# Attention with keys on the partitions: scores made transposed, row maxima from a separate one-pass product, denominators added up on GpSimd

## The reference, cut to what matters

```python
def block_attention(q, k, v):          # latent: 8 query heads, 2 key heads, head size 64, 2048 + 128 keys
    scale = HEAD_DIM ** -0.5
    def one_block(qblk):               # 128 queries
        s = jnp.einsum('bkgqd,bskd->bkgqs', qblk, k).astype(jnp.float32) * scale
        p = jax.nn.softmax(s, axis=-1).astype(v.dtype)
        return jnp.einsum('bkgqs,bskd->bkgqd', p, v)
```

## Time and profile before

| | |
|---|---|
| median of three runs | 3549.56 us |
| the profiled execution, its time | 3547.59 us |
| its span in the profile | 3545.8 us |
| TensorE busy, span | 3171.3 us (89%) |
| VectorE busy, span | 1878.6 us (53%) |
| ScalarE busy, span | 1671.7 us (47%) |
| GpSimd busy, span | 388.6 us (11%) |
| mean granted clock of TensorE | 0.939 of full speed |

### The profile page before, as it was taken

One profiled execution on the slowest core, in us unless ns is written; L12 is line 12 of the kernel. 1 busy time (PEld: TensorE's weight loads), 2 busy tenths in 40 slices (PEclk: granted clock), 3 DMA queues, 4 the chain that ended last, 5 costly groups with the idle time before them and its releaser, 6 DMA issues. The chain is left out here.

```text
span 3545.8 us, 60756 instructions
## 1 busy us (share of the span) xinstructions
PE 3171.3 (89%) x21856; PEld 2900.2 (82%) x21856; DVE 1878.6 (53%) x3485; ACT 1671.7 (47%) x3239; POOL 388.6 (11%) x400
## 2 busy tenths in 40 slices
PE   6999994759999999999699756999999999999991
PEld 6788883748888888888588645999999999999991
DVE  2222226548888888888533365545455445545443
ACT  2222220547777777777434202455455544455442
POOL 0333333500000000000000000010010000110001
PEclk9999997869999999999799855999999999999996
DMA  5121113410000000000244204565565555665545
GB/s 217 43 80 60 67 66 116 140 42 25 27 27 27 27 27 27 27 27 27 81 147 150 83 0 132 174 192 185 179 198 184 183 187 179 188 193 181 181 130 220
DMA packets 307599, 393.69 MB, mean 111 GB/s; under 512 B 13808, under 2 KB 263872, under 8 KB 306496
## 3 DMA queue, kind: packets, MB, share of 16 engines
q1 hardware_dynamic: 293680, 338.64, 28.9%
q0 software_dynamic: 10240, 35.66, 4.4%
q10 hardware_dynamic: 3600, 18.35, 1.3%
HBM read 318.68 MB, written 74.06 MB: 111 GB/s over the span
## 5 line engine op out<-in xcount | busy, mean ns | idle before, releaser
L2304 DVE TENSOR_TENSOR e_w_lo<-e_raw,e_w_hi 128x2048 fp32r<-128x2048 f32 x192 | 440.1, 2292 | 490.4 <-ACT e_w_hi L2246 490.4
L92 PE MATMUL e_ps<-e_x_hi,e_w_hi 128*128 128x272 f32 x2048 | 602.1, 294 | 5.5 <-issue 5.5
L94 PE MATMUL e_ps<-e_x_hi,e_w_lo 128*128 128x272 f32 x2048 | 593.8, 290 | 0.0
L93 PE MATMUL e_ps<-e_x_lo,e_w_hi 128*128 128x272 f32 x2048 | 590.1, 288 | 0.0
L2246 ACT ACTIVATE e_w_hi<-e_raw 128x2048 fp32r<-128x2048 f32 x192 | 366.1, 1907 | 163.7 <-DMA e_raw<-in_w_gate 159.3
L1470 DVE TENSOR_TENSOR a_pT_lo<-a_ps_t,a_pT_hi 128x512 fp32r<-128x512 f32 (+1 forms) x648 | 368.0, 601 | 139.5 <-ACT a_pT_hi L1368 139.2
L1368 ACT ACTIVATE a_pT_hi<-a_ps_t 128x512 fp32r<-128x512 f32 (+1 forms) x648 | 319.6, 532 | 185.1 <-PE a_ps_t L1238 180.5
L92 PEld LDWEIGHTS e_ps<-e_x_hi,e_w_hi 128*128 128x128 f32 x2048 | 386.1, 189 | 7.1 <-issue 5.5
L93 PEld LDWEIGHTS e_ps<-e_x_lo,e_w_hi 128*128 128x128 f32 x2048 | 386.9, 189 | 0.0
L94 PEld LDWEIGHTS e_ps<-e_x_hi,e_w_lo 128*128 128x128 f32 x2048 | 385.8, 188 | 0.0
L1443 DVE TENSOR_REDUCE a_mx<-a_ps_s 128x1 f32<-128x896 f32 (+2 forms) x392 | 346.1, 890 | 26.8 <-PE a_ps_s L1228 26.8
(11 more groups left out here) (269 smaller groups left out, 5478.2 us busy)
## 6 DMA issues: line engine op xcount, KB each, us to landing
e_raw<-in_w_gate SPq DMA_DIRECT2D x64, 1024.0 KB, 5.2
e_raw<-in_w_up SPq DMA_DIRECT2D x64, 1024.0 KB, 5.2
e_raw<-in_w_down SPq DMA_DIRECT2D x64, 1024.0 KB, 5.2
a_wm<-in_w_mod SPq DMA_DIRECT2D x32, 512.0 KB, 4.0
s_ret<-p_pr SPq DMA_DIRECT2D x17, 768.0 KB, 3.6
m_raw<-in_w_in ACTq DMA_DIRECT2D x8, 1152.0 KB, 7.1
o_cT<-s_ct SPq DMA_DIRECT2D x17, 512.0 KB, 4.7
s_x<-o_x SPq DMA_DIRECT2D x17, 512.0 KB, 4.9
```

The lines of the kernel that those rows point to most:

```text
L92: nc.tensor.matmul(out, w_hi, x_hi, start=first, stop=False)
L93: nc.tensor.matmul(out, w_hi, x_lo, start=False, stop=False)
L94: return nc.tensor.matmul(out, w_lo, x_hi, start=False, stop=last)
L2304: nc.vector.tensor_tensor(w_lo[n % RING][:, :, :], raw[n % RING][:, :, :], w_hi[n % RING][:, :, :].bitcast(F32), ALU.subtract).then_inc(w_ ...
```

## The change

The probabilities are now made with keys on the partitions, so nothing has to be transposed. The unit of work becomes a slot: one query tile and one key head, hence 4 heads times 128 queries = 512 columns (`QCOLS`). There are two slots in a tile. The 17 key tiles of a slot are taken in 9 pairs (`PAIRS`), the last of one tile only.

- `scores` uses a key tile as weights and 512 query columns as the moving side: two matmuls of 512 columns per key tile, one with k_hi over 128 rows, one with k_lo over 64 rows and a 65th row. That row is 1 in `keys_lo` and minus the query's maximum in `qM`, so the subtraction of the maximum is part of the sum, and `exps` needs no bias.
- The maximum must be known beforehand. `rough` makes one-pass scores (k_hi alone) with queries on the partitions, in 20 pieces of 448 or 384 columns per slot (`PIECE_W`), in two banks `ps_r`. VectorE reduces each (`maxima`), then the pieces (`tops`); TensorE turns the maxima into a row (`turn_top`), and ScalarE copies it with its sign changed (`keep_top`). All this runs one slot ahead, `PIECES_IN` pieces beside each pair.
- `exps` writes 128x1024 probabilities into a ring of three buffers (`prob`), `high` rounds them into `p_hi` on ScalarE, `low` writes the remainder to `p_lo` on VectorE. Both inputs of `low` are in SBUF.
- The denominators come from GpSimd: `add` sums the probabilities of all pairs into `acc` (seven instructions of 1024 columns, two of 512 a slot), and four small products with a column of ones in `fold_halves` finish the sum.
- `value` has 512 columns. All side work goes through one PSUM bank, `ps_m`.
- In the key loop ScalarE copies tile i - 1 (`keep_keys`, now two copies) after it has rounded tile i. Queries are loaded and split before the key loop.

```diff
-SEG_ORDER = [0, 2, 1]
-PIECES = [(0, 3), (3, 6), (6, 9), (9, 12), (12, 15), (15, KEY_TILES)]
-GROUP = 2
-NGRP = NQ // GROUP
+PAIRS = (KEY_TILES + 1) // 2
+PIECE_W = [448, 448, 448, 448, KEY_TILES * P - 4 * 448]
+PIECES = len(PIECE_W) * QPK
+PIECES_IN = [0, 3, 3, 3, 3, 3, 3, 2, 0]
+QCOLS = QPK * P
+QUADS = NKV * NT
+RING = 3
...
+            def add(i, v, r, out, x, y):
+                n = pair(i, v, 0) + r
+                if r:
+                    pool.wait_ge(folded, n)
+                nc.gpsimd.tensor_tensor(out, x, y, ALU.add).then_inc(folded, 1)
+
+            def body(i):
+                for v in range(NKV):
+                    pool.wait_ge(exped, pair(i, v, 1) + 1)
+                    add(i, v, 0, acc[:, :, :], prob[:, 0, :, :], prob[:, 1, :, :])
+                    for j in range(2, PAIRS - 1):
+                        pool.wait_ge(exped, pair(i, v, j) + 1)
+                        add(i, v, j - 1, acc[:, :, :], acc[:, :, :], prob[:, j % RING, :, :])
+                    if not first_slot(i, v):
+                        pool.wait_ge(filled, use_of_fold(*before(i, v)) + 1)
+                    add(i, v, PAIRS - 2, acc_all[:, :], acc[:, 0, :], acc[:, 1, :])
+                    pool.wait_ge(exped, pair(i, v, PAIRS - 1) + 1)
+                    add(i, v, PAIRS - 1, acc_all[:, :], acc_all[:, :], prob[:, (PAIRS - 1) % RING, 0, :])
+
+            slots(pool, body)
 
         @block.tensor
...
+            def rough(i, v, n):
+
+                if n == 0:
+                    pe.wait_ge(emptied, use_of_queries(i, v) + 1)
+                if not (first_slot(i, v) and n < 2):
+                    pe.wait_ge(max_ok, piece(i, v, n) - 1)
+                h, part = (n, 0) if ctx_tile(i) else (n // len(PIECE_W), n % len(PIECE_W))
+                w = P if ctx_tile(i) else PIECE_W[part]
+                src = CTX_KEYS * P if ctx_tile(i) else sum(PIECE_W[0:part])
+                nc.tensor.matmul(ps_r[n % 2][:, 0:w], qT[v][:, h * P:(h + 1) * P], keys[:, v, src:src + w],
+                                 start=True, stop=True).then_inc(rough_ok, 1)
...
+            def scores(i, v, j, t):
+
+                n = pair(i, v, j)
+                b = (v + j) % 2
+                if j == 0 and t == 0:
+                    pe.wait_ge(emptied, use_of_top(i, v) + 1)
+                    pe.wait_ge(qM_ok, quad(i, v) + 1)
+                if t == 0 and not (first_slot(i, v) and j < 2):
+                    pe.wait_ge(exped, n - 1)
+                src = CTX_KEYS if ctx_tile(i) else 2 * j + t
+                nc.tensor.matmul(ps_s[b][:, t, :], keys[:, v, src * P:(src + 1) * P], qT[v][:, :], start=True, stop=False)
+                ins = nc.tensor.matmul(ps_s[b][:, t, :], keys_lo[:, v, src * P:(src + 1) * P], qM[v][:, :],
+                                       start=False, stop=True)
+                if t == tiles_of(i, j)[-1]:
+                    ins.then_inc(scored, 1)
+
...
+            def slot(i, v):
+                last, ahead = before(i, v), following(i, v)
+                at = 0
+                for j in range(PAIRS):
+                    todo = list(range(at, min(at + PIECES_IN[j], pieces_of(ahead[0]))))
+                    at = at + PIECES_IN[j]
+                    if j == 0:
+                        if not first_slot(i, v):
+                            for t in range(2):
+                                value(*last, PAIRS - 2, t)
+                        turn_queries(*ahead)
+                    for t in tiles_of(i, j):
+                        scores(i, v, j, t)
+                        if todo:
+                            rough(*ahead, todo.pop(0))
+                    if j == PAIRS - 1:
+                        turn_top(*ahead)
+                    if j == 1 and not first_slot(i, v):
+                        value(*last, PAIRS - 1, 0)
+                    for t in range(2):
+                        if j >= 2:
+                            value(i, v, j - 2, t)
+                        if todo:
+                            rough(*ahead, todo.pop(0))
+                    if j == 2:
+                        modulation(i, v)
+                    if j == 3 and not first_slot(i, v):
+                        fold_halves(*last)
+                    if j == 5 and not first_slot(i, v):
+                        turn_out(*last)
 
             def body(i):
-                bank = Bank(i)
-                for h in range(NQ):
-                    uses_before = [bank.uses_of(b) for b in range(2)]
-                    for kind, n in step_events(i, h):
-                        if kind == "q":
-                            turn_queries(i + 1, n, bank)
...
+            def exps(i, v, j):
+
+                n = pair(i, v, j)
+                act.wait_ge(scored, n + 1)
+                if not (first_slot(i, v) and j < RING):
+                    act.wait_ge(lo_ok, PAIRS * (QUADS - 1) + 7 + v if ctx_tile(i) else n - RING + 1)
+                    done = {0: PAIRS * quad(*before(i, v)) + 6, 1: PAIRS * quad(*before(i, v)) + 7,
+                            2: PAIRS * quad(*before(i, v)) + 9}[j] if j < RING and not ctx_tile(i) else \
+                        PAIRS * (QUADS - 1) + 6 + v if ctx_tile(i) else PAIRS * quad(i, v) + max(j - RING, 1)
+                    act.wait_ge(folded, done)
+                m = len(tiles_of(i, j))
...
+            def high(i, v, j):
+
+                n = pair(i, v, j)
+                act.wait_ge(exped, n + 1)
+                if ctx_tile(i):
+                    act.wait_ge(valued, PAIRS * (QUADS - 1) + v + 1)
+                elif not first_slot(i, v):
+                    act.wait_ge(valued, n - PAIRS + 1)
+                m = len(tiles_of(i, j))
+                nc.scalar.activation(p_hi[:, place(i, v, j), 0:m, :], prob[:, place(i, v, j) % RING, 0:m, :], ACT.Copy)\
+                    .then_inc(hi_ok, 1)
...
+            def maxima(i, v, n):
+
+                dve.wait_ge(rough_ok, piece(i, v, n) + 1)
+                h, part = (n, 0) if ctx_tile(i) else (n // len(PIECE_W), n % len(PIECE_W))
+                w = P if ctx_tile(i) else PIECE_W[part]
+                nc.vector.reduce_max(mx[:, h, part:part + 1], ps_r[n % 2][:, 0:w], AX).then_inc(max_ok, 1)
+
+            def tops(i, v):
+
+                dve.wait_ge(max_ok, piece(i, v, pieces_of(i)))
+                if first_slot(i, v):
+                    dve.wait_ge(made, 2)
+                else:
+                    dve.wait_ge(filled, use_of_top(*before(i, v)) + 1)
+                n = 1 if ctx_tile(i) else len(PIECE_W)
+                nc.vector.reduce_max(top[:, :, HD:HD + 1].rearrange("p h o -> p (h o)"), mx[:, :, 0:n], AX).then_inc(top_ok, 1)
+
...
+            def low(i, v, j):
+
+                dve.wait_ge(hi_ok, pair(i, v, j) + 1)
+                m = len(tiles_of(i, j))
+                at = place(i, v, j)
+                nc.vector.tensor_tensor(p_lo[:, at, 0:m, :], prob[:, at % RING, 0:m, :], p_hi[:, at, 0:m, :].bitcast(F32),
+                                        ALU.subtract).then_inc(lo_ok, 1)
+
...
+            def slot(i, v):
+                last, ahead = before(i, v), following(i, v)
+                at = 0
+                for j in range(PAIRS):
+                    todo = list(range(at, min(at + PIECES_IN[j], pieces_of(ahead[0]))))
+                    at = at + PIECES_IN[j]
+                    if j == 3:
+                        keep_modulation(i, v)
+                    if j == 4 and not first_slot(i, v):
+                        combine(*last)
+                    if todo:
+                        maxima(*ahead, todo.pop(0))
+                    if j == 7:
+                        if todo:
+                            maxima(*ahead, todo.pop(0))
+                        tops(*ahead)
+                    if j:
+                        low(i, v, j - 1)
+                    elif not first_slot(i, v):
+                        low(*last, PAIRS - 1)
+                    for n in todo:
+                        maxima(*ahead, n)
+                    if j == 0:
+                        copy_queries(*ahead)
+                    if j == 4 and v == 0:
+                        queries_lo(i + 1)
 
```

641 lines of the change are left out of this document (280 added, 361 removed).

## The result

The changed kernel takes 3751.18 us (median of four runs, 3725.79 to 3772.18). The kernel before takes 3548.57 beside it, so the ratio is 1.057, 95% interval 1.0483 to 1.0657. The direction was as forecast. The size was not: 3597 us was expected, with 3680 as the upper end.

What follows compares the result with a forecast made beforehand. GpSimd additions and VectorE subtractions, excluding each other, were taken to bound a slot: 14.5 + 32 x 31.9 + 13 = 1048 us against 984.6, +64; key loop -14; +50 on 3547.6 gives 3597 us, range 3560 to 3635, reaching to 3515 and 3680.

Steps and rivals of the forecast that it cites:

- slots, 32: Attention's main part: 32 slots of 31.9 us each, against 29.6 for half a query tile before.
- prologue: From attention's last key copy to the first real scores: 14.5 us with nothing beside it, bounds 10 to 18.
- epilogue: End of attention with the context tile: three chains from value to copy, 4.4 us each, 13 us, bounds 10 to 18.
- key loop: Attention's loop over 16 key tiles: 1.9 us a tile instead of 2.84, so -14 us, bounds 0 and -20.
- rival B: In attention TensorE, 75% busy with gaps, runs a third of the slots' time at clock 0.50: 3680 us; 14%.
- the exchange: In slots, GpSimd additions and VectorE subtractions exclude each other: 30.8 - 2.1 + 3.2 = 31.9 us; 59%.
- the queue behind a blocked subtraction: In a slot, maxima wait behind the subtraction, then TensorE's rough products (two banks only), scores and values; no separate size.
- signs: In attention: POOL near 70%, adds 2.4 to 3.5 us, `a_p_lo` shortest 1.22, mean well above 1.7, TensorE clock 1.00.
- the queries' subtraction: VectorE's subtraction for new queries: half of it, 0.35 us, counted in each slot's sum.
- TensorE's own work: Per slot 24 us: 15.4 for 68 products of 512 columns, up to 4.5 rough products, about 4.5 side work.
- Rival A: In slots, no exclusion that counts: VectorE bounds a slot at 28 us, total 3472 us; 20%.

Runs made afterwards that it cites:

- e1: The changed kernel with GpSimd's additions cut to one column each, denominators left out: 3574.34 us, ratio 1.007.
- e5: e1 with seven unused 512-column products filling TensorE's long wait before the fourth rough product: 3494.44 us, ratio 0.985.
- e7: The changed kernel with three of TensorE's waits filled by products that change nothing (9, 7 and 5 of 512 columns): 3643.39 us, ratio 1.026.
- e4: The changed kernel with exponentials in place in the PSUM score buffer, subtraction reading one operand there, GpSimd adding only rounded parts: 3549.63 us, ratio 1.000.
- e2: The changed kernel with each GpSimd addition replaced by a one-column one and an SBUF fill of about equal length: 3577.49 us, ratio 1.008.
- e8: e4 with modulation products moved to the end of pair 1 and, in pair 7, VectorE's subtraction before its last two maxima and tops: 3464.23 us, ratio 0.976.
- e11: e4 with only the modulation products moved to the end of pair 1, VectorE's order in pair 7 kept: 3479.07 us, ratio 0.981.
- e10: The changed kernel with only the 16 modulation products moved from the end of pair 2 to pair 1: 3677.47 us, ratio 1.037.

## Why the prediction was wrong

The profiled executions differ by 3725.8 - 3547.6 = 178 us; the forecast was 50. Term by term:

| term | predicted us | measured us | off by |
|---|---|---|---|
| slots, 32 | 32 x 31.9 = 1021 | 1129.3 | +108 |
| of it at full clock | 31.9 | (31.4 + 33.7) / 2 = 32.55 | +21 |
| of it the half clock | 0 | 35.29 - 32.55 = 2.74 a slot | +88 |
| prologue | 14.5 | 761.0 - 742.9 = 18.1 | +4 |
| epilogue | 13 | 1920.1 - 1890.3 = 29.8 | +17 |
| key loop | -14 | 742.9 - 760.0 = -17.1 | -3 |

The sum of the last column without the two rows "of it", +126, and the forecast of 3597 make 3723 us; 3726 was measured.

**The step that failed: TensorE's clock.** The sum took all slots at clock 1.00, and the half clock stood apart as rival B with 14%. It was no alternative to the exchange; both came at once. VectorE's maxima and remainders come late, TensorE has two banks of rough scores and then stands for 1.2 to 2.6 us, and the clock falls. The exchange makes these waits more and longer, but e1 has one of 1.7 us and 5.4 us a slot at half clock without any exchange. e5 and e7 show the cause: filling the waits alone took nearly all of the half clock away, and 80 and 108 us with it. I argued from the mean busy share of a stage (75%), with a later stage at 73% and clock 0.50 and another at 62% and 0.99 as evidence for both sides. The question was where the idle time lies. The prediction had even named the queue behind a blocked subtraction (maxima, then rough products, then scores) and left it out of the price. B's own price, 0.33 x 8 = 2.6 us a slot and 85 us in all, nearly meets the 2.7 and 88 measured, but by luck: it had a third of the time at half clock, which is 22%, and 8 us for a slot of 40 wholly at half clock, 0.20 for each such us, where 2.74 / 7.9 = 0.35 was paid. The median is 25 us above the profiled execution; executions at 3771 have a mean clock of 0.90 against 0.909, so it goes with the clock as well.

**The exchange: right in kind, nearly right in size.** 31.9 us against 32.55. All its signs came but TensorE's clock of 1.00: subtractions of 1.22 in the shortest and 3.42 in the longest, mean 1.74 (just above the 1.7 named); adds of 2.36 to 3.45 (and the first add of 512 columns 2.07 to 2.14, where e4 has it at 1.28); TensorE's idle time in front of rough products and values released by `a_mx` and `a_p_lo`; GpSimd busy for 62% (70% was expected, of shorter slots). Slots with `v` = 0 are 2.3 us longer than the others; 0.35 was allotted for the queries' subtraction in the mean, but it waits for an add (1.84 us), and the next subtraction stands again behind it (2.86). By the Trainium skill (SBUF — State Buffer, "Who interferes with whom") a VectorE instruction with two SBUF inputs contends with a GpSimd one that reads SBUF and not with one that only writes it; the runs agree, with up to 3.42 us against the adds and never over 1.23 against e2's fills. With one input in PSUM (e4) it was never over 1.23 against whole adds either. (The old kernel's subtraction for the queries has both operands in SBUF too, which the prediction overlooked; GpSimd did nothing beside it.)

**TensorE's own work was 2.2 to 2.7 us too small.** 24 us a slot were predicted. Slots of e8 take 26.7 and 27.25 at full clock, 0.5 of it waiting. The side work (4.4 us for 4.5) and the rough products (4.3) were right; the 68 wide ones take 17.5 us for 15.4 in a slot of 26.7, with a median step of 0.233 us, and 13 of 0.31 to 0.45. It did no harm to the sum, because the exchange was longer.

**Rival A** had the right slot at full clock (28.0; e1 has 28.4) and the wrong total (3472; 3574), for the same reason as the forecast.

**Prologue and epilogue** are chains of one engine waiting for the next, the first wholly at half clock, the second mostly (0.63 in the mean): 20 rough products and maxima at 0.75 us each in place of 0.54, and in the epilogue 6.0 us before the next queries are turned (the last slot's blocked subtractions), then one `a_attT` copy each 6 to 8 us where 4.4 was estimated. **The key loop** was right: two tiles in 731.83 - 728.16 = 3.67 us, 1.84 each for 1.9. ScalarE's timeline:

```profile
728.16 0.42 ACT L1347 ACTIVATE a_k_hi<-a_kv_row 128x256 fp32r<-128x256 f32 x1 [0.76 <-DMA a_kv_row<-s_kv]
...
731.83 0.42 ACT L1347 ACTIVATE a_k_hi<-a_kv_row 128x256 fp32r<-128x256 f32 x1 [0.73 <-DMA a_kv_row<-s_kv]
```

It stays open why the fall follows one such wait and not another (12 of e1's 26 have none), and which of e8's falls could still be had; nothing was tried on the epilogue.

## What to carry to other kernels

Before work is put on GpSimd, look where VectorE's operands lie while it runs: one of them in PSUM made nearly the same adds free for it here, worth 5%. When a change makes TensorE idle for parts of a stage, don't take the mean share: find its single waits (here of 1.2 to 2.6 us), and count half clock after them as part of the price (here up to 0.35 us for each us of it). The cheapest repair tried here is to move needed TensorE work into such a wait: it gave 71 us in e11 and 74 in e10.
